# Finding an expert's rows in one-pass weights, the first expert's row numbers first, an early fetch that nothing uses, and the last statistics placed elsewhere in the queue

## The chip, the cores and the metric

One core of one Trainium2 chip. The metric is the device time of one launch in microseconds (us), median of the runs. TensorE multiplies, VectorE (DVE), ScalarE (ACT) and GpSimd (POOL) do the rest, SyncE (SP) issues most DMAs. Each engine runs its own list of instructions in order and waits on semaphores.

## What is computed

One step of a two-layer decoder trunk over 272 prompt positions (16 meta tokens and 256 new ones) and 32 sample tokens, all in float32, width 1024. Layer 0: pooling mixer and dense SwiGLU. Layer 1: conformer convolution and top-2-of-8 SwiGLU. Each sub-layer ends in a layer norm of 4**0.25 * x + f(x). The part that the change touches is the last sub-layer, for the 288 rows (256 prompt, 32 sample) that are handed out:

```
logits = xf @ router                       # (288, 8)
top_v, top_i = top_k(logits, 2); probs = softmax(top_v)
gate[t, e] = probability of expert e for row t, 0 if not chosen
y = sum over e of gate[:, e:e+1] * swiglu(xf, wg[e], wu[e], wd[e])
out = layer_norm(4**0.25 * xf + y)
```

## The kernel before

The work is laid out by hand: five engine programs, each a fixed order of instructions, tied by counting semaphores. Weights come in 1 MB tiles into a ring of eleven buffers (`raw`). ACT copies each tile into a rounded high part (`hi(t)`, L683) and DVE forms the low part (`lo(t)`, L1334), so that a product of float32 numbers is three matmuls on operands of type fp32r (L1075, L1106, L1243, L1267).

**Routing.** DVE takes the two largest of eight logits (`top_v`, `top_i`), makes masks `pick1`, `pick2`, `taken`, and TensorE counts with triangular matrices where each row stands in the list of its expert (L1196). `slot_of` holds this place. `select(e0, e1)` (L1648) compares it with 0 to 127 and writes for experts e0 to e1 a 0/1 matrix `sel` (rows by places). `find_rows` (L1211) multiplies `sel` with `gate`, which holds per row a one, the eight shares and the row's number, in float32: ten columns for each expert, three matmuls for each expert (rows in parts of 128, 128 and 32), in three groups `FINDS` (expert 0; 1 to 3; 4 to 7). `input_rows(k)` (L1658, L1660) copies row numbers into `row_in` and the rest into `found`; `output_rows` (L1678 to L1685) makes from it the shares and the rows to add to. Eight narrow-purpose matmuls in `mean_mat` follow (`keep_busy(8)`, L999, each two instructions in the trace).

**The first fetch.** POOL waits until the 288 rows are in DRAM (`rows_stored`, L507) and until `row_in` has expert 0's numbers, and fetches its rows by an indirect DMA (L616) into `xg_rows`. TensorE, once its own list has come to it, turns them (`gather_turn`, L1221), ACT and DVE split them (`xg_hi` L889, `xg_lo` L1715), and the first expert's matmuls start (L1243).

**An expert** has 33 tiles, in six blocks j = 0 to 5 (NB = 6). For each block TensorE multiplies by gate tiles, turns the hidden block j-1 (`turn_h`, L1252), multiplies by up tiles, and runs `down(j-1)` (L1267), which waits for DVE's `turn_low(j-1)` (`ht_lo`, L1739). Blocks 0 to 4 have two gate tiles, two up tiles and two down tiles; block 5 has one of each. `down(5)` stands behind all six blocks. DVE's order in block j is: two `lo` tiles, `turn_low(j-1)`, two `lo` tiles, `mult(j)` (`hn`, L1734), two `lo` tiles.

**The end.** All rows but those of expert 7 are finished while expert 7 runs. SP loads the sums of experts 0 to 6 into `acc` (L517, three DMAs, counted to 48 by `sums_loaded`), behind the last weight tiles and the rows of gains and biases. DVE, in expert 7, behind the last `lo` of block 4, waits for the 48 and does for the three parts of the rows `rows_stats` (L1692, L1695), then in block 5 `turn_low(4)`, `rows_center` (L1700) of two parts, `mult(5)`, the third centre, `rows_scale` (L1709) of two parts, `turn_low(5)` and the third scale. `last_rows` (L1789 to L1801) does the rows of expert 7, which POOL places in the outputs.

Of the kernel before, what the change touches and what calls it, by code (L numbers as in the profile page):

```python
# [24 lines left out]
F32 = mybir.dt.float32  # L25
# [15 lines left out]
def build_trunk(nc, x_prompt, x_sample, state_pool, state_conv, meta, pool_w, pool_scale, conv_w1,  # L41
# [57 lines left out]
    with ExitStack() as ctx:  # L99
# [40 lines left out]
        GC = E + 2  # L140
        gate = const("gate", [P, 3, GC])
        slot_of = const("slot_of", [P, 3, E + 1])
        trash = const("trash", [P, 2])
# [67 lines left out]
        sel = area("sel", [P, E, 3, P], F32, M0 + 12288)  # L211
# [9 lines left out]
        xg_lo = area("xg_lo", [P, KC, P], F32R, M1 + 4096)  # L221
        hn = area("hn", [P, BW], F32, M1 + 8192)
# [12 lines left out]
        found = area("found", [P, 1 + E * (GC + 1)], F32, 8576)  # L235
# [8 lines left out]
        def sem(name):  # L244
            return ctx.enter_context(nc.semaphore(name))
# [85 lines left out]
        rows_moved = sem("rows_moved")  # L331
        found_moved = sem("found_moved")
# [75 lines left out]
        FINDS = ((0, 1, 4), (1, 4, 5), (4, E, 6))  # L408
# [172 lines left out]
        def _(pool):  # L581
# [17 lines left out]
            pool.memset(gate[:], 0.0).then_inc(pool_step, 1)  # L599
# [5 lines left out]
            pool.memset(gate[:, :, 0:1], 1.0).then_inc(consts_ready, 1)  # L605
            pool.iota(gate[:, :, GC - 1:GC], pattern=[[P, 3], [1, 1]], base=0, channel_multiplier=1,
# [43 lines left out]
            with pool.If(largest > P):  # L650

                pool.indirect_dma_start(sums_dram, rows(row_out[:, E - 1:E], 0), yy[:], None).then_inc(added, 16)
                for r in (1, 2):
                    pool.wait_ge(in_ready, r * 3 + 3)
# [10 lines left out]
        N_CONSTS = 13  # L665
# [314 lines left out]
        def _(pe):  # L980
# [223 lines left out]
            def find_rows(r, k):  # L1204

                e0, e1, bank = FINDS[k]
                pe.wait_ge(sel_ready, r * len(FINDS) + (k + 1))
                for e in range(e0, e1):
                    for i in range(3):
                        n = OUT_ROWS[i]  # L1210
                        last = pe.matmul(ps[bank][:, GC * e:GC * (e + 1)], sel[0:n, e, i, :], gate[0:n, i, :],  # L1211
                                         start=(i == 0), stop=(i == 2))
                last.then_inc(rows_found, 1)
# [108 lines left out]
        def _(dve):  # L1322
# [28 lines left out]
            link(dve.tensor_scalar(recip[:], slot_no[:, 0:16], 1.0, None, ALU.add))  # L1351
            link(dve.reciprocal(recip[:], recip[:]))
# [277 lines left out]
            dve.wait_ge(placed, 1)  # L1630
            for i in range(3):
                last = dve.tensor_scalar(pick1[:, i, :], pick1[:, i, :], prob[:, i, 2:3], None, ALU.mult)
            link(last)
            for i in range(3):
                last = dve.scalar_tensor_tensor(out=slot_of[:, i, 0:E], in0=ps[1][:, i * E:(i + 1) * E], scalar=1.0,
                                                in1=taken[:, i, :], op0=ALU.add, op1=ALU.mult)
            for i in range(3):
                n = OUT_ROWS[i]
                last = dve.scalar_tensor_tensor(out=gate[0:n, i, 1:1 + E], in0=pick2[0:n, i, :],
                                                scalar=prob[0:n, i, 3:4], in1=pick1[0:n, i, :],  # L1640
                                                op0=ALU.mult, op1=ALU.add)
# [13 lines left out]
            def input_rows(k):  # L1655
                e0, e1, bank = FINDS[k]
                cols = slice(GC * e0, GC * e1)
                dve.tensor_copy(row_in[:, e0:e1], ps[bank][:, cols].rearrange("p (e c) -> p e c", c=GC)[:, :, GC - 1])\  # L1658
                    .then_inc(in_ready, 1)
                dve.tensor_copy(found[:, cols], ps[bank][:, cols]).then_inc(found_moved, 1)  # L1660
# [10 lines left out]
            for k in (1, 2):  # L1671
                dve.wait_ge(rows_found, k + 1)
                input_rows(k)

            def output_rows(r):

                dve.wait_ge(found_moved, r * len(FINDS) + len(FINDS))
                dve.tensor_scalar(row_f[:], found_at[:, :, 0], trash[:, 1:2], trash[:, 0:1], ALU.mult,  # L1678
                                  ALU.add).then_inc(rows_moved, 1)
                dve.tensor_copy(share[:], found[:, 1:].rearrange("p (e c) -> p e c", c=GC + 1)[:, :, 0])\  # L1680
                    .then_inc(rows_moved, 1)
# [37 lines left out]
            def one_expert(r, first, side, last):  # L1719
# [22 lines left out]
                for j in range(NB):  # L1742
                    a = FIRST[j] + AHEAD
                    ahead(a)
                    if halves(j) == 2:
                        ahead(a + 1)
                    if j:
                        turn_low(j - 1)
                    if halves(j) == 2:
                        ahead(a + 2)  # L1750
                        ahead(a + 3)
                    else:
                        ahead(a + 1)
# [9 lines left out]
                    if kept and j == NB - 2:  # L1763
                        dve.wait_ge(sums_loaded, 48)
                        for i in range(3):
# [59 lines left out]
            xg_low(0)  # L1825
            one_pass(0)
# [3 lines left out]
            with dve.If(largest > P):  # L1830
                dve.wait_ge(y_placed, 32)
                with dve.Fori(1, 3) as r:
# [7 lines left out]
                    for k in range(len(FINDS)):  # L1840
                        dve.wait_ge(rows_found, r * len(FINDS) + (k + 1))
                        input_rows(k)
# [41 lines left out]
```

## Time and profile before

| what | value |
|---|---|
| median of 3 runs | 1248.1 us (1248.07 to 1249.15) |
| the profiled execution's own time | 1249.45 us |
| its span, first to last instruction | 1247.7 us |
| TensorE busy / share of the span | 1206.4 us / 97% |
| VectorE, ScalarE, GpSimd busy | 975.4, 807.1, 31.9 us |
| mean granted TensorE clock | 0.989 |
| chain that ended last | PE 87%, DVE 9%, ACT 2%, DMA 1%, issue 1% |

The span is 1.75 us short of that execution's own time. TensorE is nearly always busy in the profile, but a busy TensorE may be one at a low clock or with very narrow operands, and the chain of what ended last leaves TensorE at places where another engine holds it up.

### The profile page before, as it was taken

The page shows a single profiled execution, that of the slowest core. Times are in us where ns is not written, and L with a number is a line of the kernel's source. Part 1 is how long each engine was busy: PE and PEld are TensorE (multiplying, and loading weights), DVE is VectorE, ACT ScalarE, POOL GpSimd, SP SyncE. Part 2 cuts the span into 40 slices and gives each one's busy share as a digit, 9 for nine tenths or more (in the row PEclk, how much of TensorE's full clock was granted, in tenths as well). Part 3 has the DMA queues.
Part 4 walks back from the last instruction along what each step waited for, and adds up shares of the span by engine and source line. Part 5 has one row for each costly group of instructions (what it writes and reads, how often), then busy time and mean ns, then how long its engine had stood idle before and what let it go on. Part 6 is the DMA issues. An engine that isn't in the chain of part 4 may idle for free.

```text
span 1247.7 us, 16144 instructions
## 1 busy us (share of the span) xinstructions
PE 1206.4 (97%) x6567; PEld 1045.6 (84%) x6567; DVE 975.4 (78%) x907; ACT 807.1 (65%) x875; POOL 31.9 (3%) x40
## 2 busy tenths in 40 slices
PE   6999999999998989999999999999999999999996
PEld 4899999999997878888888888888888888888885
DVE  6787444447898559889888888888888888888887
ACT  4545654436596448768767777777777777777771
POOL 0000000000000000001001001001001001001000
PEclk9999999999999979999999999999999999999998
DMA  9144544442193439999999999999999999999991
GB/s 257 41 151 153 169 145 160 141 156 90 53 318 107 135 110 327 366 366 359 385 371 359 388 368 356 393 374 358 391 367 348 394 376 342 394 380 344 395 345 50
DMA packets 171388, 345.74 MB, mean 277 GB/s; under 512 B 7042, under 2 KB 59618, under 8 KB 171274
## 3 DMA queue, kind: packets, MB, share of 16 engines
q1 hardware_dynamic: 168515, 335.34, 75.1%
q0 software_dynamic: 2592, 8.66, 2.8%
q8 instruction: 54, 0.88, 0.3%
q10 hardware_dynamic: 199, 0.62, 0.2%
q14 instruction: 28, 0.23, 0.1%
HBM read 336.34 MB, written 10.44 MB: 278 GB/s over the span
## 4 chain that ended last, share of the span: by engine, by line
PE 87%; DVE 9%; ACT 2%; DMA 1%; issue 1%; POOLq 0%; ACTq 0%; POOL 0%; DVEq 0%
PE bank L1243 39%; PE bank L1267 19%; PE bank L1075 18%; PE bank L1106 6%; DVE cacc L1517 3%; PE bank L1252 1%; PE bank L1014 1%; PE bank L1211 1%; DVE w_lo L1334 1%; DMA spool<-in_state_pool_dram 1%; PE bank L1060 1%; DVE sg L1414 1%; ACT w_hi L683 0%; ACT sq L727 0%; DVE cacc L1538 0%
## 5 line engine op out<-in xcount | busy, mean ns | idle before, releaser
L1334 DVE TENSOR_TENSOR w_lo<-raw,w_hi 128x2048 fp32r<-128x2048 f32 x309 | 704.5, 2290 | 164.8 <-ACT w_hi L683 163.8
L683 ACT CAST w_hi<-raw 128x2048 fp32r<-128x2048 f32 x309 | 589.5, 1916 | 243.2 <-PE bank L1243 81.3
L1243 PE MATMUL bank<-w_hi,xg_hi 128*128 128x512 f32 (+1 forms) x768 | 292.1, 380 | 1.1 <-DVE xg_lo L1715 1.1
L1243 PE MATMUL bank<-w_hi,xg_lo 128*128 128x512 f32 (+1 forms) x768 | 288.6, 376 | 0.0
L1243 PE MATMUL bank<-w_lo,xg_hi 128*128 128x512 f32 (+1 forms) x768 | 288.6, 376 | 0.0
L1075 PE MATMUL bank<-x_hi,w_hi 128*128 128x304 f32 (+1 forms) x544 | 166.8, 307 | 6.9 <-DVE x_lo L1421 3.7
L1243 PEld LDWEIGHTS bank<-w_hi,xg_hi 128*128 128x128 f32 x768 | 144.2, 188 | 29.2 <-issue 1.3
L1243 PEld LDWEIGHTS bank<-w_hi,xg_lo 128*128 128x128 f32 x768 | 144.2, 188 | 29.1
L1243 PEld LDWEIGHTS bank<-w_lo,xg_hi 128*128 128x128 f32 x768 | 144.4, 188 | 28.0
L1075 PE MATMUL bank<-x_lo,w_hi 128*128 128x304 f32 (+1 forms) x544 | 165.1, 304 | 0.0
L1075 PE MATMUL bank<-x_hi,w_lo 128*128 128x304 f32 (+1 forms) x544 | 164.5, 302 | 0.0
L1267 PE MATMUL bank<-w_hi,ht_hi 128*128 128x512 f32 x352 | 140.1, 398 | 1.7 <-DVE ht_lo L1739 1.4
L1267 PE MATMUL bank<-w_hi,ht_lo 128*128 128x512 f32 x352 | 139.2, 395 | 0.0
L1267 PE MATMUL bank<-w_lo,ht_hi 128*128 128x512 f32 x352 | 139.1, 395 | 0.0
L1075 PEld LDWEIGHTS bank<-x_hi,w_hi 128*128 128x128 f32 x544 | 103.2, 190 | 8.8 <-issue 6.3
L1075 PEld LDWEIGHTS bank<-x_hi,w_lo 128*128 128x128 f32 x544 | 103.2, 190 | 0.0
L1075 PEld LDWEIGHTS bank<-x_lo,w_hi 128*128 128x128 f32 x544 | 103.0, 189 | 0.1
L1267 PEld LDWEIGHTS bank<-w_hi,ht_hi 128*128 128x128 f32 x352 | 66.0, 188 | 19.1 <-DVE ht_lo L1739 3.8
L1267 PEld LDWEIGHTS bank<-w_hi,ht_lo 128*128 128x128 f32 x352 | 66.0, 188 | 16.1
L1267 PEld LDWEIGHTS bank<-w_lo,ht_hi 128*128 128x128 f32 x352 | 66.0, 188 | 15.3
L1106 PE MATMUL bank<-h_hi,w_hi 128*128 128x304 f32 x176 | 54.5, 310 | 1.9 <-DVE h_lo L1491 1.9
L1517 DVE SCALAR_TENSOR_TENSOR cacc<-uext,vec,cacc 128x256 f32<-128x256 f32 x134 | 53.9, 480 | 0.0
(206 smaller groups left out, 1097.0 us busy)
## 6 DMA issues: line engine op xcount, KB each, us to landing
raw<-in_moe_w_gate_dram SPq DMA_DIRECT2D x88, 1024.0 KB, 7.0
raw<-in_moe_w_up_dram SPq DMA_DIRECT2D x88, 1024.0 KB, 7.4
raw<-in_moe_w_down_dram SPq DMA_DIRECT2D x88, 1024.0 KB, 7.1
raw<-in_conv_w_dram SPq DMA_DIRECT2D x12, 1024.0 KB, 5.2
raw<-in_ffn_w_gate_dram SPq DMA_DIRECT2D x11, 1024.0 KB, 5.3
raw<-in_ffn_w_up_dram SPq DMA_DIRECT2D x11, 1024.0 KB, 5.3
raw<-in_ffn_w_down_dram SPq DMA_DIRECT2D x11, 1024.0 KB, 4.8
sums_dram<-acc SPq DMA_DIRECT2D x3, 512.0 KB, 3.0
```

Source lines behind the costliest of these rows:

```text
L683: act.copy(w_hi[t % HIGH][:], raw[raw_slot(t)][:]).then_inc(hi_ready, 1)
L1014: last = pe.matmul(ps[0][:, 0:n], mean_mat[:], z(c), start=(c == first), stop=(c == end))
L1060: last = pe.matmul(ps[1][:, 0:n], mean_mat[:], sq[:, c, 0:n], start=(c == 0), stop=(c == KC - 1))
L1075: last = pe.matmul(bank[:, 0:n], w[:, c, cols], x[:, c, 0:n], start=(c == 0 and k == 0), stop=(c == KC - 1 and k == 2))
L1106: last = pe.matmul(ps[c][:, 0:NT], w[:, s, cols], x[i % 2][:, s, :], start=(i == 0 and s == 0 and k == 0), stop=(i == NJ - 1 and s == TR - ...
L1211: last = pe.matmul(ps[bank][:, GC * e:GC * (e + 1)], sel[0:n, e, i, :], gate[0:n, i, :], start=(i == 0), stop=(i == 2))
L1243: done = pe.matmul(bank[:, 0:w], x[:, f, :], m[:, c, :], start=(f == 0 and k == 0), stop=(f == KC - 1 and k == 2))
L1252: done = pe.transpose(ps[4 + j % 2][:, s * P:(s + 1) * P], hn[:, s * P:(s + 1) * P], ident[:])
L1267: done = pe.matmul(ps[6 + half][:, :], x[:, i * TR + s, :], w[:, s, cols], start=(j == 0 and i == 0 and s == 0 and k == 0), stop=(j == NB ...
L1334: dve.tensor_tensor(w_lo[raw_slot(t)][:], raw[raw_slot(t)][:], w_hi[t % HIGH][:], ALU.subtract).then_inc(split_ready, 1)
L1414: link(dve.reciprocal(rs[:, 0:n], rs[:, 0:n]))
L1517: ins = dve.scalar_tensor_tensor(out=out, in0=src, scalar=v(V_DW + KC * k + q), in1=out, op0=ALU.mult, op1=ALU.add)
```

## The change

`gate` with its ten columns becomes `row_cols` with 18 columns of type fp32r: a one, the eight shares rounded, the eight remainders of the shares, and the row's number. `sel` is fp32r too, so `find_rows` multiplies fp32r by fp32r. `FINDS` has two groups of four experts. Ahead of them three matmuls of two columns (the row's number and its neighbour) find expert 0's row numbers alone. DVE no longer forms the shares before `slot_of`; it scales `pick1` before it waits for the places, forms `gate`, the rounded parts and the remainders between the first `select` and the others, and copies `row_in` for experts 1 to 7 in one go once both groups are found. `keep_busy(8)` becomes `keep_busy(4)`, behind a wait for `in_ready`. POOL fetches 128 rows of the prompt into an area that nothing reads (`hn_all`), once the statistics of the last norm ahead of the routing are done; DVE waits for its landing before the experts. At the start POOL writes one more constant and DVE copies the row numbers into `row_cols`. In expert 7 DVE waits for the sums, and does `rows_stats` of part 0, ahead of `turn_low(3)`; part 1 stands ahead of `mult(4)`; part 2 and the centres of parts 0 and 1 stand at the end of block 4; the centre of part 2 stands ahead of `mult(5)`, and all three scales ahead of `turn_low(5)`.

```diff
-        GC = E + 2
-        gate = const("gate", [P, 3, GC])
+        GC = 2 * E + 2
+        row_cols = const("row_cols", [P, 3, GC], F32R)
-        sel = area("sel", [P, E, 3, P], F32, M0 + 12288)
+        sel = area("sel", [P, E, 3, P], F32R, M0 + 12288)
-        FINDS = ((0, 1, 4), (1, 4, 5), (4, E, 6))
+        FINDS = ((0, E // 2, 5), (E // 2, E, 6))
...
+            pool.wait_ge(var_done, 4)
+            pool.indirect_dma_start(hn_all[:], None, x_prompt[0], rows(any_row[:], 0)).then_inc(warmed, 16)
             pool.wait_ge(rows_stored, 48)
             pool.wait_ge(in_ready, 1)
             fetch(0, 0)
-            pool.wait_ge(in_ready, 3)
+            pool.wait_ge(in_ready, 2)
...
-                pe.wait_ge(sel_ready, r * len(FINDS) + (k + 1))
+                pe.wait_ge(sel_ready, r * len(FINDS) + (k + 2))
...
+            pe.wait_ge(sel_ready, 1)
+            for i in range(3):
+                n = OUT_ROWS[i]
+                last = pe.matmul(ps[1][:, 0:2], sel[0:n, 0, i, :], row_cols[0:n, i, GC - 2:GC],
+                                 start=(i == 0), stop=(i == 2))
+            last.then_inc(first_found, 1)
             for k in range(len(FINDS)):
                 pe.wait_ge(acc_ready, FINDS[k][2] - 2)
                 find_rows(0, k)
-            keep_busy(8, bank=1)
+            pe.wait_ge(in_ready, 1)
+            keep_busy(4, bank=1)
...
-            dve.wait_ge(placed, 1)
             for i in range(3):
                 last = dve.tensor_scalar(pick1[:, i, :], pick1[:, i, :], prob[:, i, 2:3], None, ALU.mult)
             link(last)
+            dve.wait_ge(placed, 1)
...
             select(0, 1)
-            select(1, 4)
             dve.wait_ge(turned, T_XJ + len(X_JOBS))
-            dve.wait_ge(rows_found, 1)
-            input_rows(0)
-            select(4, E)
+            for i in range(3):
+                n = OUT_ROWS[i]
+                last = dve.scalar_tensor_tensor(out=gate[0:n, i, :], in0=pick2[0:n, i, :], scalar=prob[0:n, i, 3:4],
+                                                in1=pick1[0:n, i, :], op0=ALU.mult, op1=ALU.add)
+            last.then_inc(gate_step, 1)
+            dve.wait_ge(first_found, 1)
+            dve.tensor_copy(row_in[:, 0:1], ps[1][:, 1:2]).then_inc(in_ready, 1)
+            dve.wait_ge(gate_step, 1)
+            dve.tensor_copy(row_cols[:, 0:2, 1:1 + E], gate[:, 0:2, :])
+            dve.tensor_copy(row_cols[0:NS, 2, 1:1 + E], gate[0:NS, 2, :]).then_inc(gate_step, 1)
+            dve.wait_ge(gate_step, 2)
+            dve.tensor_tensor(row_cols[:, 0:2, 1 + E:1 + 2 * E], gate[:, 0:2, :], row_cols[:, 0:2, 1:1 + E], ALU.subtract)
+            dve.tensor_tensor(row_cols[0:NS, 2, 1 + E:1 + 2 * E], gate[0:NS, 2, :], row_cols[0:NS, 2, 1:1 + E],
+                              ALU.subtract).then_inc(gate_step, 1)
+            dve.wait_ge(gate_step, 3)
+            select(1, E // 2)
+            select(E // 2, E)
...
+                    if kept and j == NB - 2:
+                        dve.wait_ge(sums_loaded, 48)
+                        rows_stats(0, 0)
                     if j:
                         turn_low(j - 1)
...
+                    if kept and j == NB - 2:
+                        rows_stats(0, 1)
                     if kept and j == NB - 1:
-                        for i in range(2):
-                            rows_center(0, i)
+                        rows_center(0, 2)
                     mult(j)
...
                     if kept and j == NB - 2:
-                        dve.wait_ge(sums_loaded, 48)
-                        for i in range(3):
-                            rows_stats(0, i)
+                        rows_stats(0, 2)
                         dve.wait_ge(rows_landed, 32)
+                        for i in range(2):
+                            rows_center(0, i)
                 if kept:
-                    rows_center(0, 2)
-                    for i in range(2):
+                    for i in range(3):
                         rows_scale(0, i)
                 turn_low(NB - 1)
-                if kept:
-                    rows_scale(0, 2)
```

## Rows read from the trace of the kernel before

**Rows 1.** Chain of waits, 380 to 472 us: start us, us, engine, tile, line.
```profile
452.37 10.40 PE bank L1211 x42
462.78 3.42 PE bank L999 x16
...
468.12 3.97 PE bank L1243 x16
```

**Rows 2.** Timeline, 436 to 475 us: start us, us, engine, line, operation, tiles, [idle before].
```profile
447.91 0.17 DVE L1629 TENSOR_TENSOR prob<-prob 128x3 f32<-128x3 f32 x1
...
448.91 0.50 DVE L1632 TENSOR_SCALAR pick<-pick,prob 128x8 f32<-128x8 f32 x3 [0.83 <-PE bank L1196]
449.44 0.31 DVE L1635 SCALAR_TENSOR_TENSOR slot_of<-bank,taken 128x8 f32<-128x8 f32 x3
449.67 0.48 DVE L1639 SCALAR_TENSOR_TENSOR gate<-pick,prob,pick 128x8 f32<-128x8 f32 x3
...
450.40 1.83 DVE L1648 TENSOR_TENSOR sel<-slot_no,slot_of 128x384 f32<-128x384 f32 x2
...
451.10 0.90 PE L1211 MATMUL bank<-gate,sel 128*128 128x10 f32 x6 [1.45 <-DVE sel L1648]
452.14 0.15 DVE L1658 CAST row_in<-bank 128x1 uint32<-128x1 f32 x1
...
453.19 1.84 POOL L616 DMA_INDIRECT xg_rows<-rows_dram,row_in  x1 [169.06 <-DVE row_in L1658]
...
467.84 0.95 POOL L616 DMA_INDIRECT xg_rows<-rows_dram,row_in  x1 [12.80 <-PE bank L1221]
```

**Rows 3.** DMA issues, 452 to 462 us: queue, KB each, us from issue to landing.
```profile
xg_rows<-rows_dram,row_in POOLq DMA_INDIRECT x1, 5.3
```

**Rows 4.** Windows, routing: length, busy per engine, TensorE clock, DMA share, GB/s.
```profile
436.00:444.00 8.00, 6.61 (x39) 3.58 (x38) 7.84 (x11) 5.12 (x11) 0.00 (x0) 1.00 0.00 0
...
452.00:463.00 11.00, 10.63 (x44) 10.28 (x44) 2.71 (x10) 0.00 (x0) 1.84 (x1) 0.50 0.47 158
463.00:466.00 3.00, 3.00 (x16) 3.00 (x16) 0.79 (x5) 0.00 (x0) 0.00 (x0) 0.54 0.00 0
```

**Rows 5.** Windows, the convolution on TensorE: the same columns.
```profile
360.00:370.00 10.00, 10.00 (x87) 10.00 (x86) 10.00 (x32) 10.00 (x35) 0.00 (x0) 1.00 0.89 313
```

**Rows 6.** Windows, an idle stretch and the work behind it: the same columns.
```profile
46.70:48.50 1.80, 0.00 (x0) 0.02 (x1) 1.63 (x4) 0.99 (x2) 0.00 (x0) 1.00 0.01 5
49.40:52.60 3.20, 3.20 (x15) 3.20 (x14) 3.20 (x8) 1.83 (x4) 0.00 (x0) 0.50 0.00 0
```

**Rows 7.** Timeline of VectorE, last expert.
```profile
1207.74 2.29 DVE L1334 TENSOR_TENSOR w_lo<-raw,w_hi 128x2048 fp32r<-128x2048 f32 x1 [0.51 <-ACT w_hi L683]
1209.94 0.68 DVE L1739 TENSOR_TENSOR ht_lo<-bank,ht_hi 128x512 fp32r<-128x512 f32 x1
...
1215.97 0.68 DVE L1734 TENSOR_TENSOR hn<-sgn,bank 128x512 f32<-128x512 f32 x1
...
1221.56 1.28 DVE L1692 BATCH_NORM_STATS2 stats<-acc 128x6 f32<-128x512 f32 x2
...
1225.78 0.64 DVE L1739 TENSOR_TENSOR ht_lo<-bank,ht_hi 128x512 fp32r<-128x512 f32 x1
1226.34 2.47 DVE L1700 SCALAR_TENSOR_TENSOR acc<-acc,mv,g_row 128x1024 f32<-128x1024 f32 x2
```

**Rows 8.** Timeline of TensorE, last expert.
```profile
1214.36 0.40 PE L1267 MATMUL bank<-w_hi,ht_hi 128*128 128x512 f32 x1
...
1226.47 0.50 PE L1267 MATMUL bank<-w_hi,ht_hi 128*128 128x512 f32 x1 [0.31 <-DVE ht_lo L1739]
...
1233.64 0.50 PE L1267 MATMUL bank<-w_hi,ht_hi 128*128 128x512 f32 x1 [1.06 <-DVE ht_lo L1739]
```

**Rows 9.** Timeline of the SyncE queue, last expert.
```profile
1204.38 1.56 SPq L517 DMA_DIRECT2D acc<-sums_dram  x3
```

**Rows 10.** DMA issues, 1200 to 1210 us: queue, KB each, us from issue to landing.
```profile
acc<-sums_dram SPq DMA_DIRECT2D x1, 128.0 KB, 9.7
```

More of the change, by code:

```diff
@@ L234, in build_trunk @@
         stats = area("stats", [P, 4, 2, 6], F32, 8384)
-        found = area("found", [P, 1 + E * (GC + 1)], F32, 8576)
+        gate = area("gate", [P, 3, E], F32, 9280)
+        found = area("found", [P, 1 + E + E * (GC + 1)], F32, 8576)
+        assert 8576 + 4 * (1 + E + E * (GC + 1)) <= 9280
         rows_dram = nc.dram_tensor("rows_dram", (NM, D), F32, kind="Internal").ap()
@@ L331, in build_trunk @@
         rows_moved = sem("rows_moved")
+        warmed = sem("warmed")
+        first_found = sem("first_found")
+        gate_step = sem("gate_step")
         found_moved = sem("found_moved")
@@ L598, in _ @@
                 pool.memset(t[:], 0.0 if t is not slot_of else NEG).then_inc(consts_ready, 1)
-            pool.memset(gate[:], 0.0).then_inc(pool_step, 1)
+            pool.iota(any_row[:], pattern=[[1, 1]], base=0, channel_multiplier=1).then_inc(consts_ready, 1)
+            pool.memset(row_cols[:].bitcast(F32), 0.0).then_inc(pool_step, 1)
             pool.iota(trash[:, 0:1], pattern=[[1, 1]], base=NM, channel_multiplier=1,
@@ L604, in _ @@
             pool.wait_ge(pool_step, 3)
-            pool.memset(gate[:, :, 0:1], 1.0).then_inc(consts_ready, 1)
-            pool.iota(gate[:, :, GC - 1:GC], pattern=[[P, 3], [1, 1]], base=0, channel_multiplier=1,
+            pool.memset(row_cols[:, :, 0:1].bitcast(F32), 1.0).then_inc(consts_ready, 1)
+            pool.iota(trash[:, 2:5], pattern=[[P, 3]], base=0, channel_multiplier=1,
                       allow_small_or_imprecise_dtypes=True).then_inc(consts_ready, 1)
@@ L1210, in find_rows @@
                         n = OUT_ROWS[i]
-                        last = pe.matmul(ps[bank][:, GC * e:GC * (e + 1)], sel[0:n, e, i, :], gate[0:n, i, :],
+                        last = pe.matmul(ps[bank][:, GC * e:GC * (e + 1)], sel[0:n, e, i, :], row_cols[0:n, i, :],
                                          start=(i == 0), stop=(i == 2))
@@ L1636, in _ @@
                                                 in1=taken[:, i, :], op0=ALU.add, op1=ALU.mult)
-            for i in range(3):
[L1638 to L1641, printed above, removed]
             link(last)
@@ L1653, in _, with found_share @@
             found_row = found_at[:, :, GC - 1]
[L1655 to L1660, printed above, removed]
+            def found_share(c):
+                return found[:, c:c + E * (GC + 1)].rearrange("p (e c) -> p e c", c=GC + 1)[:, :, 0]
             select(0, 1)
-            select(1, 4)
             dve.wait_ge(turned, T_XJ + len(X_JOBS))
-            dve.wait_ge(rows_found, 1)
-            input_rows(0)
-            select(4, E)
+            for i in range(3):
[15 more added lines that the diff above has]
+            select(E // 2, E)
             dve.wait_ge(counted, 1)
@@ L1670, in _ @@
             dve.tensor_copy(most_i[:], most[:]).then_inc(flag_ready, 1)
-            for k in (1, 2):
-                dve.wait_ge(rows_found, k + 1)
-                input_rows(k)
+            dve.wait_ge(rows_found, 1)
+            dve.tensor_copy(found[:, 0:GC * (E // 2)], ps[5][:, 0:GC * (E // 2)]).then_inc(found_moved, 1)
+            dve.wait_ge(rows_found, 2)
+            dve.tensor_copy(found[:, GC * (E // 2):GC * E], ps[6][:, GC * (E // 2):GC * E]).then_inc(found_moved, 1)
+            dve.wait_ge(found_moved, 2)
+            dve.tensor_copy(row_in[:, 1:E], found_row[:, 1:E]).then_inc(in_ready, 1)
             def output_rows(r):
@@ L1679, in output_rows @@
                                   ALU.add).then_inc(rows_moved, 1)
-                dve.tensor_copy(share[:], found[:, 1:].rearrange("p (e c) -> p e c", c=GC + 1)[:, :, 0])\
-                    .then_inc(rows_moved, 1)
+                dve.tensor_tensor(share[:], found_share(1), found_share(1 + E), ALU.add).then_inc(rows_moved, 1)
                 dve.wait_ge(rows_moved, r * 3 + 2)
@@ L1839, in _ @@
                         select(e0, e1)
-                    for k in range(len(FINDS)):
+                    for k, (e0, e1, bank) in enumerate(FINDS):
                         dve.wait_ge(rows_found, r * len(FINDS) + (k + 1))
-                        input_rows(k)
+                        dve.tensor_copy(found[:, GC * e0:GC * e1], ps[bank][:, GC * e0:GC * e1]).then_inc(found_moved, 1)
+                    dve.wait_ge(found_moved, r * len(FINDS) + len(FINDS))
+                    dve.tensor_copy(row_in[:], found_row).then_inc(in_ready, 2)
                     output_rows(r)
```

11 lines of the change are left out of this document (7 added, 4 removed).

## The prediction, made before the changed kernel had run

> **What bounds the kernel now.** I read the page's busy shares first (TensorE 97%), then the chain of waits, to see at which places TensorE's time is not the matmuls of the weights. Two such places meet the change.
>
> The first is the routing. The chain there [rows 1] is all TensorE: 42 instructions of finding rows take 10.40 us, 16 of keep-busy 3.42, then the turn of the fetched rows, and the experts start at 468.12. The finds have ten columns, so they carry next to no work, yet they take 10.40 / 42 = 0.248 us each. The windows say why they are that slow: the granted clock is 0.50 from 452 to 463 us and 0.54 in the next three [rows 4], the lower level, 1.2 GHz, where the convolution ran at 1.00 [rows 5]. The first fetch is no bound: POOL starts it at 453.19 [rows 2] and it lands 5.3 us later [rows 3], at 458.5, while TensorE comes to the turn only at 462.78 + 3.42 = 466.2.
>
> The second is expert 7. TensorE waits for DVE's `turn_low` twice, 0.31 and 1.06 us [rows 8]. DVE's timeline [rows 7] is full: what DVE is given there, or made to wait for, goes on to TensorE. Between these two places lie seven experts bound by TensorE, which a shift passes through unchanged, so the two effects add.
>
> **The routing, step by step.** `pick1` is now scaled before the wait for `placed`. DVE's last step ahead of it ended at 447.91 + 0.17 = 448.08 and the scale takes 0.50, so it is done before 448.91, when the places came [rows 2]: 449.44 - 448.91 = 0.53 gone. `gate` leaves the stretch too, 0.4 of its 0.48. The first `select` starts 0.93 sooner, at 449.47. Finding started 0.70 behind it (451.10), so now at 450.17, and its three matmuls instead of six instructions end some 0.4 sooner than the 1.04 that passed until `row_in` (452.14). `row_in` is written at 450.8, POOL starts the fetch 1.05 later as before (453.19 - 452.14), at 451.85, and it lands by 457.2 even at the old 5.3.
>
> The warming fetch starts near 434, once the last norm's statistics are done. POOL has nothing to do then, and from 436 to 444 us the DMAs move nothing [rows 4]; that is its cover, and without it half a megabyte would cost about what the fetch costs, 5 us of a queue that nobody waits for. What it can give is the issue, 1.84 us for the first fetch and 0.95 for the second [rows 2]. That is 0.9 on a fetch that has 460.4 - 457.2 = 3 us of slack behind TensorE. I cost it at nothing; below nothing is excluded by the same slack.
>
> DVE then has two casts and two subtractions of 8 or 16 columns, like its small steps of 0.15 to 0.18: 0.5 us with the links, so `select` of experts 1 to 3 starts at 451.4. A pair of selects for four experts took 1.83, 0.46 each, so they are ready at 452.8 and those of 4 to 7 at 454.6. TensorE now starts the main finds at 452.9.
>
> How long they take the trace doesn't show: no fp32r matmul of few columns is in it. The number of instructions falls from 48 to 24 (plus three), since fp32r goes in one where float32 takes two, as [rows 2] has six for three calls. Each is bounded by 0.115 us from below (the convolution, 87 in 10 us at the full clock [rows 5]) and 0.248 from above. At the low clock, which I expect to last (TensorE has even less to do here), twice 0.115 is 0.23, and both rows meet: I take 0.24. So 24 x 0.24 = 5.8, finds end at 458.7; eight instructions of keep-busy at 3.42 / 16 = 0.214 are 1.7, 460.4. From there to the first expert matmul it took 468.12 - 466.2 = 1.9, with the clock just risen; at the low clock four of the transposes in that path take 0.4 more. The experts start at 462.7, **5.4 us sooner**. `output_rows` is done by 460, earlier than needed. At 0.115 each, DVE's selects and the fetch bind instead: turn at 457.1, experts at 459.0, 9.1 sooner. At 0.248 it is 5.2.
>
> The clock then: keep-busy ran from 462.8, and a clock of 0.54 over 463 to 466 [rows 4] means that it rose 0.24 us before the end, at 465.76: 3 us. Now it runs 1.7 and the transposes 1.7, so the clock may not have risen when the experts start. A wait behind a norm shows the price: TensorE idle at 46.7 to 48.5, the clock at 0.50 from 49.4 to 52.6 [rows 6], during which 3.2 us of matmuls do 1.6 us of work. Ends: 0, and 1.6; I take half, **+0.8**.
>
> The start: one more constant on POOL and one small copy on DVE stand in front of inputs that are still being loaded; nothing, and at most the copy's 0.15.
>
> **Expert 7, step by step.** DVE now waits for all three loads of `acc` ahead of `turn_low(3)`. When have they landed? SP issues them from 1204.38 on for 1.56 us [rows 9], behind the last weight tiles and the two rows of gains, and the last one lands 9.7 us after its issue [rows 10] at 1205.5: 1215.2. That order is unchanged. DVE comes to the wait at 1209.94 [rows 7], so it stands still for 5.3 us. Queued behind are `turn_low(3)`, for which TensorE's `down(3)` waits, due at 1214.36 [rows 8], four `lo` tiles and `mult(4)`. Counting from 1215.2: one `rows_stats` (1225.78 - 1221.56 = 4.22 for three, 1.41 each), `turn_low(3)` 0.56 to the next instruction, four `lo` at 1209.94 - 1207.74 = 2.2 each, two more `rows_stats` 2.8, `mult(4)` 0.6, two centres 2.4, and from the start of `turn_low(4)` to TensorE 1226.47 - 1225.78 = 0.7. That sums to 1.4 + 0.6 + 8.8 + 2.8 + 0.6 + 2.4 + 0.7 = 17.3: `down(4)` starts at 1232.5, where it started at 1226.47. **+6.0 us.** `down(3)` slips to 1217.3, but TensorE has slack behind it: the work up to `down(4)` took 1226.47 - 0.31 - 1214.36 = 11.8, so it is through at 1229.1. From `down(4)` to `down(5)` 1233.64 - 1226.47 = 7.2 passed, so `down(5)` is due at 1239.7. DVE meanwhile has the third centre, `mult(5)` and three scales, each of the size of a centre with a reciprocal (1.2 + 0.4 + 3 x 1.45): through at 1238.5, so `turn_low(5)` is late by nothing; it may save up to 0.2 of the old 1.06, or cost 0.3 if a scale runs over. The third scale, gone from behind `turn_low(5)`, saves nothing, since `last_rows` waits for TensorE. The step's bounds are 5.7 and 6.5, by these and by the links between pieces.
>
> TensorE idles 3 us before `down(3)` and over 3 before `down(4)`. After 1.8 us of idling the clock fell [rows 6]. If it falls here, `down(4)` and what follows run slow for up to 3.2 us, at 1.6; part of a low stretch falls into the idling. Ends 0 and 1.6, I take **+1.2**.
>
> **Sum.** -5.4 + 0.8 + 6.0 + 1.2 = +2.6. Against the profiled execution's span that is 1250.3, its own time 1252.05; the median lies 1.35 below that execution, so 1248.1 + 2.6 = **1250.7**.
>
> **The rivals.** Beside the forecast (A, chance 0.50, own range 1248.8 to 1252.8):
>
> B, quick finds (0.15): the clock is at 1.00 in them, or one costs nearer 0.115. Front -9.1, tail +6.6: 1245.6. For it: fewer instructions. Against it: the clock fell and stayed low with more of them [rows 4].
>
> C, no stall in expert 7 (0.12), the one on the other side: the three sums are there when DVE asks. Then the stats and centres move into DVE's small idle places, `down(4)` starts within 0.5 of its time, and -4.6 + 0 gives 1243.5. It decides if the last landing comes before 1209.94, 5.3 us sooner than now; at 2.6 us sooner the whole is even with before. Against it: nothing issues them sooner.
>
> D, the clock stays low on into expert 0 (0.13): the transposes of the gather don't bring it up, and keep-busy is too short, so it rises only on expert matmuls, another 3.2 us at half speed, +1.6: 1252.3. For it: in 10.40 us of finds it never rose, though TensorE was busy 0.97 of the time [rows 4], so being busy is not enough. The Trainium skill, "TensorE: Matmul & The Clock Gate", Part 4: PE-mode transpose, says that transposes don't count as TensorE being busy in the way matmuls do; by it only the 1.7 us of keep-busy would help. The trace has no clock that rises on transposes alone, nor one that fails to.
>
> E, two passes in fp32r too (0.05): 48 x 0.248 = 11.9, experts start 0.6 later than before, +7.8: 1255.9. The weights' matmuls, once in the records for each call, speak against it.
>
> The rest, 0.05, is anything else, both ways.
>
> **Range and chances.** Under 0.2% (2.5 us) nothing can be told from no change. Leaving out C and E and a little more: 1245.6 to 1253.2. Slower: 0.30 of A, all of D and E, 0.02 of the rest, 0.50. Faster: C, 0.05 of B and 0.01, 0.18. Within: 0.32.
>
> **What would show it.** Right: 27 finds in one instruction each near 0.24 us at clock 0.50; POOL's fetch about 1.3 us sooner and 0.95 long; the first L1243 near 462.7; DVE idle some 5 us in expert 7 until the sums land; `down(4)` idle by over 3 us. Wrong: finds at 0.12 us, sums that land before DVE asks, or a first expert at half clock for many matmuls.

## The result and the profile after

The changed kernel took 1254.88 us, the median of four runs (1253.32 to 1257.67), against 1248.09 of before (1247.98 to 1249.15, four runs). The ratio is 1.0051, 95% interval 1.0038 to 1.0063: slower by half a percent. The profiled execution was the quickest of the four, 1253.32 us with a span of 1251.6; that of before had 1249.45 and 1247.7. The forecast was 1250.7, slower, and the time lies 1.7 us above its range. The two places that it named are there: expert 7 with the size that it gave, the routing 1.2 us short of it. What it left out lies between them.

The routing comes first. The chain of waits in the trace of the changed kernel, 440 to 475 us (start, us, what), answers to [rows 1]:

```profile
451.53 6.71 PE bank L1222 x24
458.24 2.00 PE bank L1010 x8
460.24 0.87 PE bank L1232 x4
...
462.59 12.64 PE bank L1254 x53
```

The timeline of the same stretch answers to [rows 2], and the DMA issues to [rows 3]:

```profile
444.19 2.23 SPq L514 DMA_DIRECT2D rows_dram<-xn  x3
...
448.18 0.56 DVE L1662 TENSOR_TENSOR sel<-slot_no,slot_of 128x384 fp32r<-128x384 f32 x1
...
449.41 0.16 DVE L1681 CAST row_in<-bank 128x1 uint32<-128x1 f32 x1 [0.27 <-PE bank L1320]
...
450.35 1.85 POOL L624 DMA_INDIRECT xg_rows<-rows_dram,row_in  x1 [14.97 <-DVE row_in L1681]
...
451.53 6.71 PE L1222 MATMUL bank<-row_cols,sel 128*128 128x18 f32 x24 [2.16 <-DVE sel L1662]
```

```profile
xg_rows<-rows_dram,row_in POOLq DMA_INDIRECT x1, 6.9
```

The first expert matmul is at 462.59, 5.53 us ahead of [rows 1]. Some of that is older than the routing. The rows' store, which stands ahead of it, is issued at 444.19; in the profile of before it was at 445.48, 1.29 later:

```profile
445.48 2.23 SPq L507 DMA_DIRECT2D rows_dram<-xn  x3
```

In the profile of before the clock was low for 3.4 us near 50 us [rows 6]; in this one it was 1.00 from 49.4 to 52.6, and the product that was running there, 1056 matmuls, took 148.32 us for 149.63. So this 1.3 us is a difference of the two executions, not of the kernels. The routing itself gave 5.53 - 1.29 = 4.2 us.

The windows (length, busy time of each engine, granted clock, DMA share, GB/s) show the clock in the finds, in expert 0 and in `down(3)` of expert 7:

```profile
450.90:461.10 10.20, 9.57 (x37) 9.20 (x38) 3.63 (x11) 0.00 (x0) 1.30 (x1) 0.50 0.48 163
461.20:470.00 8.80, 7.85 (x36) 6.23 (x35) 7.12 (x5) 8.80 (x8) 0.94 (x1) 1.00 0.54 177
1215.50:1218.90 3.40, 3.40 (x9) 2.67 (x9) 3.40 (x2) 0.00 (x0) 0.00 (x0) 0.51 0.00 0
```

Then expert 7. First DVE, then TensorE, the timelines that answer to [rows 7, 8]:

```profile
1205.60 2.29 DVE L1352 TENSOR_TENSOR w_lo<-raw,w_hi 128x2048 fp32r<-128x2048 f32 x1 [0.52 <-ACT w_hi L694]
1213.09 1.28 DVE L1718 BATCH_NORM_STATS2 stats<-acc 128x6 f32<-128x512 f32 x2 [5.20 <-DMA acc<-sums_dram]
...
1214.53 0.64 DVE L1765 TENSOR_TENSOR ht_lo<-bank,ht_hi 128x512 fp32r<-128x512 f32 x1
...
1227.32 2.43 DVE L1726 SCALAR_TENSOR_TENSOR acc<-acc,mv,g_row 128x1024 f32<-128x1024 f32 x2
1229.67 0.68 DVE L1765 TENSOR_TENSOR ht_lo<-bank,ht_hi 128x512 fp32r<-128x512 f32 x1
```

```profile
1215.22 0.54 PE L1278 MATMUL bank<-w_hi,ht_hi 128*128 128x512 f32 x1 [2.81 <-DVE ht_lo L1765]
...
1230.41 0.51 PE L1278 MATMUL bank<-w_hi,ht_hi 128*128 128x512 f32 x1 [1.67 <-DVE ht_lo L1765]
...
1237.45 0.50 PE L1278 MATMUL bank<-w_hi,ht_hi 128*128 128x512 f32 x1 [0.92 <-DVE ht_lo L1765]
```

DVE stands still for 5.20 us behind the last load of the sums. `down(3)` was due at 1215.22 - 2.81 = 1212.41; `down(4)` starts 18.0 us later, where in [rows 8] it was 1226.47 - 1214.36 = 12.1: 5.9 us lost. The last wait, 0.92 for 1.06, gives 0.1 back. The clock was low in `down(3)` (0.51 in the third window), where it cost nothing: TensorE would only have waited longer for `turn_low(4)`.

The difference of the spans is 1251.6 - 1247.7 = 3.9 us. Routing and the start give -5.5, expert 7 costs +5.8. That leaves +3.6 us between them, from the first expert matmul to `down(3)` of expert 7 (1212.41 - 462.59 = 749.8 against 1214.36 - 468.12 = 746.2), which the forecast took to pass a shift through unchanged. POOL's fetches in the middle of the run, one for each expert, show it. Before:

```profile
657.44 0.99 POOL L616 DMA_INDIRECT xg_rows<-rows_dram,row_in  x1 [87.73 <-PE bank L1221]
...
753.39 0.98 POOL L616 DMA_INDIRECT xg_rows<-rows_dram,row_in  x1 [87.77 <-PE bank L1221]
```

After:

```profile
652.81 0.98 POOL L624 DMA_INDIRECT xg_rows<-rows_dram,row_in  x1 [88.19 <-PE bank L1232]
...
749.18 0.98 POOL L624 DMA_INDIRECT xg_rows<-rows_dram,row_in  x1 [88.17 <-PE bank L1232]
```

An expert takes 96.37 us where it took 95.95 (96.36 to 96.43 over the run), at a granted clock of 1.00 in both. It isn't waiting either: from 556 to 1200 us TensorE is busy for 643.66 of the 644 us, and for 643.67 in before. The matmuls themselves are slower, as the chains of waits show for a pair of gate or up tiles (L1243, now L1254) and a pair of down tiles (L1267, now L1278), 24 matmuls in a row. Before, then after:

```profile
581.55 5.59 PE bank L1243 x24
587.15 5.60 PE bank L1267 x24
```

```profile
576.55 5.62 PE bank L1254 x24
582.17 5.62 PE bank L1278 x24
```

In layer 0, and in the convolution's first product, the pace is that of before: 513 matmuls of the down product took 72.07 us for 72.06, and 384 took 54.26 for 54.28. A chip that is slower throughout doesn't explain it. In these two products the weights are the stationary operand (the one that TensorE loads ahead of a matmul); they lie ahead of the constants and did not move. The activations that stream past them did move, and cost nothing by it. In the expert matmuls it is the other way round: the activations are stationary and the weights stream.

The medians differ by 6.8 us, the two profiled executions by 3.9. Of the 2.9 between, 1.3 is the low clock near 50 us. No profile of the change shows the rest; the profiled execution is its quickest, and the experiments show two places where others of its kind lose time to the clock.

### The profile page after: what moved, and what is told of

Same layout as the page of the kernel before. It is cut to its first block, busy times and chain, and to the rows that moved or that the text cites. A ratio compares the mean times of both kernels' runs of the same rounds, so it can differ in the third digit from the quotient of the medians.

```text
span 1251.6 us, 16090 instructions
## 1 busy us (share of the span) xinstructions
PE 1205.2 (96%) x6538; PEld 1043.3 (83%) x6538; DVE 976.2 (78%) x910; ACT 807.2 (64%) x875; POOL 31.8 (3%) x42
## 4 chain that ended last, share of the span: by engine, by line
PE 86%; DVE 9%; ACT 2%; DMA 1%; issue 1%; SPq 0%; POOLq 0%; POOL 0%; DVEq 0%; ACTq 0%
PE bank L1254 38%; PE bank L1278 19%; PE bank L1086 18%; PE bank L1117 6%; DVE cacc L1536 3%; PE bank L1263 1%; DVE w_lo L1352 1%; PE bank L1025 1%; DMA acc<-sums_dram 1%; PE bank L1071 1%; DVE sg L1433 1%; PE bank L1222 1%; DMA xin<-in_x_prompt_dram 0%; ACT sq L738 0%; DVE cacc L1557 0%
## 5 line engine op out<-in xcount | busy, mean ns | idle before, releaser
L1254 PE MATMUL bank<-w_hi,xg_hi 128*128 128x512 f32 (+1 forms) x768 | 293.0, 381 | 0.9 <-DVE xg_lo L1741 0.9
L1254 PE MATMUL bank<-w_hi,xg_lo 128*128 128x512 f32 (+1 forms) x768 | 289.6, 377 | 0.0
L1254 PE MATMUL bank<-w_lo,xg_hi 128*128 128x512 f32 (+1 forms) x768 | 289.5, 377 | 0.0
L1254 PEld LDWEIGHTS bank<-w_hi,xg_hi 128*128 128x128 f32 x768 | 144.7, 188 | 29.4 <-issue 1.2
L1254 PEld LDWEIGHTS bank<-w_hi,xg_lo 128*128 128x128 f32 x768 | 144.5, 188 | 29.4
L1254 PEld LDWEIGHTS bank<-w_lo,xg_hi 128*128 128x128 f32 x768 | 144.7, 188 | 28.2
L1278 PE MATMUL bank<-w_hi,ht_hi 128*128 128x512 f32 x352 | 141.1, 401 | 5.7 <-DVE ht_lo L1765 5.4
L1278 PE MATMUL bank<-w_hi,ht_lo 128*128 128x512 f32 x352 | 140.2, 398 | 0.0
L1278 PE MATMUL bank<-w_lo,ht_hi 128*128 128x512 f32 x352 | 140.1, 398 | 0.0
L1278 PEld LDWEIGHTS bank<-w_hi,ht_hi 128*128 128x128 f32 x352 | 66.7, 189 | 23.8 <-DVE ht_lo L1765 8.3
L1278 PEld LDWEIGHTS bank<-w_hi,ht_lo 128*128 128x128 f32 x352 | 66.8, 190 | 16.2
L1278 PEld LDWEIGHTS bank<-w_lo,ht_hi 128*128 128x128 f32 x352 | 66.7, 189 | 15.6
```

Source lines behind the costliest of these rows:

```text
L1254: done = pe.matmul(bank[:, 0:w], x[:, f, :], m[:, c, :], start=(f == 0 and k == 0), stop=(f == KC - 1 and k == 2))
L1278: done = pe.matmul(ps[6 + half][:, :], x[:, i * TR + s, :], w[:, s, cols], start=(j == 0 and i == 0 and s == 0 and k == 0), stop=(j == NB ...
```

## The experiments

Two theories stood at the outset. **Place in SBUF:** the change makes the constants larger (18 columns for ten and one more constant; the three more columns of `trash` fit into its padding), in all 128 bytes for each partition, and every tile laid out behind them moves up by that, the gathered rows and the turned hidden blocks among them, which the expert matmuls have as stationary operands. **Chip or run:** the longer period belongs to the chip that ran it. Beside these, the forecast's two places had to be shown apart. Each line of the table is a kernel against the runs of before in the same job.

| kernel | median us | ratio to before, 95% interval | expert period us |
|---|---|---|---|
| the change | 1254.88 | 1.0051 (1.0038 to 1.0063) | 96.37 |
| e1_front_only | 1249.23 | 1.0001 (0.9992 to 1.0010) | 96.37 |
| e2_tail_only | 1256.23 | 1.0048 (1.0034 to 1.0062) | 96.00 |
| e3_pad128 | 1252.21 | 1.0024 (1.0014 to 1.0035) | 96.37 |
| e4_after_packed | 1252.21 | 1.0025 (1.0015 to 1.0034) | 95.97 |
| e5_front_packed | 1244.98 | 0.9964 (0.9950 to 0.9977) | 95.95 |
| e6_xg_up128 | 1250.04 | 1.0006 (0.9997 to 1.0016) | 96.16 |
| e7_front_aligned | 1245.13 | 0.9965 (0.9951 to 0.9978) | 95.76 to 95.99 |
| e8_sums_later | 1249.07 | 0.9994 (0.9985 to 1.0003) | 96.00 |
| e9_no_warming | 1245.63 | 0.9971 (0.9962 to 0.9980) | 95.95 |
| e10_keep8 | 1246.20 | 0.9980 (0.9971 to 0.9989) | 95.95 |
| e11_finds_fp32 | 1250.15 | 1.0007 (0.9998 to 1.0016) | 95.97 |

Before was 1248.09 us beside the change, 1249.2 (24 runs) beside e1 to e4, 1249.5 (21 runs) beside e5 to e8 and 1248.59 (27 runs) beside e9 to e11. So kernels of different jobs are compared by their ratios. Periods are differences of fetch starts in each kernel's profile.

**e1_front_only: the change with expert 7's old order.**

```diff
-                    if kept and j == NB - 2:
-                        dve.wait_ge(sums_loaded, 48)
-                        rows_stats(0, 0)
                     if j:
                         turn_low(j - 1)
```
(and the other statistics, the centres and the scales back where they were)

> The changed kernel with expert 7's order of before put back; the routing part alone. Theory 'two places': the changed kernel's trace has the first expert matmul 5.5 us sooner, of which 1.3 are a low clock near 50 us that its run did not have, so the routing gives about 4.3, and expert 7's wait for the sums costs it back. By that theory this kernel loses no time in expert 7 (down(4) idles 0.3, down(5) about 1 us) and is 4 us faster than before, 1244, if the experts take 95.94 us each. Rival 'slower experts': the changed kernel's experts take 96.41 each where they took 95.94; if that comes with the routing part (its larger constants move every tile behind them by 128 bytes), it takes 8 x 0.46 = 3.7 back and this kernel is at 1247.5 to 1248.

Measured 1.0001, period 96.37: the rival. In its profile the first expert matmul is at 462.91, so the gain of the routing is there, and the slower experts eat it.

**e2_tail_only: before with expert 7's new order**, the same lines the other way round.

> The kernel before with the new order of statistics, centres and scales in expert 7 alone. Theory 'two places': DVE idles 5 us for the sums, down(3) starts some 3 us late, down(4) up to 6 us late: +4 (as in the changed kernel's trace: 15.0 us from down(3)'s due time 1212.4 to down(4) plus the rest, against 12.1) to +7.2 with a low clock: 1252 to 1255, experts at 95.94. Rival 'the wait is hidden': within 1 us of before.

Measured 1.0048, 6.0 us by the ratio and 7.0 by the medians, period 96.00: within the forecast's +4 to +7.2, though 1256.23 lies above its 1255. The wait is not hidden. TensorE's timeline and windows of its profile say how it gets there:

```profile
1218.28 0.50 PE L1267 MATMUL bank<-w_hi,ht_hi 128*128 128x512 f32 x1 [3.30 <-DVE ht_lo L1739]
...
1233.46 0.56 PE L1267 MATMUL bank<-w_hi,ht_hi 128*128 128x512 f32 x1 [3.27 <-DVE ht_lo L1739]
...
1242.01 0.50 PE L1267 MATMUL bank<-w_hi,ht_hi 128*128 128x512 f32 x1 [0.92 <-DVE ht_lo L1739]
```

```profile
1233.60:1237.00 3.40, 3.40 (x9) 2.66 (x10) 3.19 (x6) 0.00 (x0) 0.00 (x0) 0.52 0.00 0
```

Two idle stretches of 3.3 us, and `down(4)` starts at the lower level of the clock and takes 8.55 us to `down(5)` where [rows 8] have 7.17. Its five runs lie at 1254.6 twice, 1256.2 and 1257.9 twice; the profiled one is among the slowest.

**e3_pad128: 128 unused bytes behind the constants of before.**

```diff
+        place[0] += 128
         work = place[0]
```

> The kernel before with 128 unused bytes behind its constants, so that every tile behind them lies 128 bytes higher, as in the changed kernel; nothing else. Theory 'place in SBUF': the expert period (fetch to fetch) goes from 95.94 to 96.4 and the kernel is 3.3 to 3.7 us slower, 1251.6. Rival 'another chip or run': the period stays what the kernel before has on the same chip, and the time too.

Measured 1.0024, 3 us where 3.3 to 3.7 were expected; period 96.37, where e2 has 96.00 on the same chip, and a pair of tiles as in the changed kernel:

```profile
581.24 5.62 PE bank L1244 x24
586.85 5.62 PE bank L1268 x24
```

Only addresses differ from before. The place in SBUF is the cause, and 'chip or run' is out.

**e4_after_packed: the change with its small constants in one tile.**

```diff
-        eps = const("eps", [P, 1])
+        scal = const("scal", [P, 16])
+        eps = scal[:, 0:1]
+        most = scal[:, 1:2]
+        most_i = scal[:, 2:3].bitcast(I32)
+        any_row = scal[:, 3:4].bitcast(U32)
+        trash = scal[:, 4:9]
+        std3 = scal[:, 9:14]
```
(and their own tiles gone, so that all behind the constants lies where it lay in before)

> The changed kernel with its small constants packed into one tile of 64 bytes, so that everything behind the constants lies where it lay before. Theory 'place in SBUF': expert period 95.94, 3.3 to 3.7 us less than the changed kernel, about 1250 to 1251. Rival 'another chip or run', or a cause in the routing part itself: no less than the changed kernel on this chip.

Measured 1.0025 for the change's 1.0051, period 95.97: the same 3 us from the other side (2.7 by the medians). The time itself, 1252.21, lies 1.2 above the expected 1250 to 1251.

**e5_front_packed: e4 with expert 7's old order.**

> The changed kernel with expert 7's order of before and with its small constants packed, so that all behind them lies where it lay before: the routing part with neither of the two costs found. If the parts add as measured (the front alone 1.0001 of before with its expert period at 96.37; the packing 2.7 us less at an equal kernel, period 95.96), it is 1249.2 - 2.7 to 3.3 = 1246 to 1246.5, 0.998 of before, the first version that beats both. Rival 'the parts don't add': 1249 again.

Measured 0.9964: both costs out, the gain of the routing is left, 4.5 us, 1 to 1.5 more than expected. This kernel beats both. It also showed a term of the forecast that the change's own profile had not: in its profile the clock is still low when expert 0 begins.

```profile
464.65:468.50 3.85, 3.85 (x9) 3.11 (x10) 2.66 (x2) 3.85 (x3) 0.94 (x1) 0.50 0.46 136
```

Nine matmuls in 3.85 us, 0.43 each for 0.23; the clock rises near 469.2. From the first expert matmul (464.65) to expert 1's fetch it is 95.42 us, for 93.37 in before: 2.0 us. (From fetch to fetch it is 95.31 for 93.65, 1.7, but expert 0's fetch had itself slipped behind the slow transposes.) Of the seven profiles with four keep-busy matmuls and fp32r finds (the change, e1, e4, e5, e7, e8, e9) four have this: e5, e7, e8 and e9. The kernels of e4 and e5 are the same up to expert 7, and one has it and the other not, so it comes and goes between executions.

**e6_xg_up128: in before, the gathered rows' parts alone 128 bytes off.**

```diff
-        xg_hi = area("xg_hi", [P, KC, P], F32R, M1)
-        xg_lo = area("xg_lo", [P, KC, P], F32R, M1 + 4096)
+        xg_hi = area("xg_hi", [P, KC, P], F32R, M1 + 128)
+        xg_lo = area("xg_lo", [P, KC, P], F32R, M1 + 16384 + 128)
```

> The kernel before with only the gathered rows' high and low parts, the stationary operands of the gate and up matmuls, 128 bytes off their place modulo 256; the turned hidden blocks and all else stay. Theory 'the stationary operand's place': a gate or up tile of 24 matmuls takes 5.62 or more a pair-tile where 5.59 was, 288 of an expert's 420 matmuls are of this kind, so the period grows by 0.29 of the 0.42, to 96.2, and the time by 2 us. Rival 'another tile's place (the turned hidden blocks, or what DVE and ACT write)': period 95.95, no change.

(`xg_lo` goes to free space 12288 bytes further on, so that it overlaps nothing; modulo 512 it too lies 128 bytes higher.) The period is 96.16, half of the way and a little less than the 96.2 expected, and the chain tells which half:

```profile
580.22 5.62 PE bank L1243 x24
585.84 5.59 PE bank L1267 x24
```

The matmuls with the moved tile as stationary operand (L1243) have the slow pace, those with the turned hidden blocks (L1267), which stayed, the quick one. The time, 1.0006 with an interval down to 0.9997, is too close to 1 to bear this alone; the periods agree to 0.01 us from one expert to the next, and they do.

**e7_front_aligned: e5 with this group 160 bytes up, at a multiple of 512.**

```diff
-        M1 = M0 + 36864
+        M1 = M0 + 36864 + 160
```

> The same kernel as the front part with packed constants, but with the gathered rows, the hidden blocks and their turned parts moved up by 160 bytes, so that they begin at a multiple of 512 bytes. Theory 'the stationary operand's place', if it is about rows that start off a boundary: the period falls below 95.95, perhaps by another 0.4 an expert, 3 us in all. Rival 'only two levels': 95.96 or 96.37.

No further gain in time, 0.9965 for 0.9964. The periods are 95.98 early in the run and 95.76 from 750 us on, where 24 matmuls take 5.57 or 5.58 us, quicker than in any other run shown here. Four experts at 0.2 less would be 0.8 us, which the interval of the ratio doesn't resolve. No run has a reason for the step, so 'a boundary' is neither shown nor ruled out; 95.76 is neither of the rival's two levels.

**e8_sums_later: e4 with the wait for the sums, and the first statistics, where the sums have landed.**

```diff
-                    if kept and j == NB - 2:
-                        dve.wait_ge(sums_loaded, 48)
-                        rows_stats(0, 0)
                     if j:
                         turn_low(j - 1)
...
                     if kept and j == NB - 2:
+                        dve.wait_ge(sums_loaded, 48)
+                        rows_stats(0, 0)
                         rows_stats(0, 1)
```

> The changed kernel with packed constants and in expert 7 only the wait for the sums and the first part's statistics put behind turn_low(3) and the two tiles that follow it, where the sums have landed (they land 5 us behind DVE's arrival in the changed kernel); centres and scales stay as changed. Theory 'the wait costs': DVE doesn't idle, down(3) starts on time, and of the 6 us only what the two centres ahead of turn_low(4) cost is left: down(4) starts 1.8 to 2.4 us late, so the kernel is 3.7 to 4 us faster than the changed one with packed constants (1252.2), 1248.3. Rival 'it is the order of statistics and centres, not the wait': less than 1.5 us faster.

Measured 0.9994 for 1.0025: 3.9 us back by the ratios, 3.1 by the medians, for 3.7 to 4 expected. Its timeline has the statistics without a wait, and `turn_low(4)` only behind the centres:

```profile
1214.47 1.28 DVE L1719 BATCH_NORM_STATS2 stats<-acc 128x6 f32<-128x512 f32 x2
...
1223.70 2.43 DVE L1727 SCALAR_TENSOR_TENSOR acc<-acc,mv,g_row 128x1024 f32<-128x1024 f32 x2
1226.05 0.68 DVE L1766 TENSOR_TENSOR ht_lo<-bank,ht_hi 128x512 fp32r<-128x512 f32 x1
```

`down(4)` then idles 2.12 us and starts at the low clock (TensorE's timeline, and windows with a granted clock of 0.52):

```profile
1226.79 0.80 PE L1279 MATMUL bank<-w_hi,ht_hi 128*128 128x512 f32 x1 [2.12 <-DVE ht_lo L1766]
```

```profile
1226.70:1230.20 3.50, 3.41 (x8) 2.75 (x9) 3.29 (x7) 0.00 (x0) 0.00 (x0) 0.52 0.00 0
```

So the stall is some half of expert 7's loss. The rest is 0.9994 against e5's 0.9964, 3.7 us. This profile accounts for 3.1 of it: `down(4)` starts 13.9 us behind `down(3)` for 12.1 in [rows 8], with the centres ahead of `turn_low(4)`, and `down(5)` 8.49 behind `down(4)` for 7.17, at the low clock. No run moves the centres alone.

**e9_no_warming: e5 without the warming fetch.**

```diff
-            pool.wait_ge(var_done, 4)
-            pool.indirect_dma_start(hn_all[:], None, x_prompt[0], rows(any_row[:], 0)).then_inc(warmed, 16)
```
(and DVE's wait for it)

> The routing part with packed constants and expert 7's order of before (0.9964 of before), without the warming fetch and DVE's wait for it; nothing else. In the changed kernel's trace the first fetch that counts took 1.85 us to issue, as in before, so the warming fetch gave nothing; TensorE has slack over its landing anyway. Theory 'no effect': issue still 1.85 us, time within 1 us of the version with it, 1245 to 1246. Rival 'it warms something': issue longer than 1.85 us, later landing, a slower kernel.

No effect: 0.9971 for 0.9964, with intervals that overlap. The first fetch takes 1.93 us to issue without it and 1.85 with it, the next one 0.94 in both:

```profile
451.36 1.93 POOL L625 DMA_INDIRECT xg_rows<-rows_dram,row_in  x1 [167.61 <-DVE row_in L1680]
...
463.60 0.94 POOL L625 DMA_INDIRECT xg_rows<-rows_dram,row_in  x1 [10.31 <-PE bank L1231]
```

**e10_keep8: e5 with `keep_busy(8)`.**

> The same routing part with eight keep-busy matmuls instead of four. They cost eight more instructions at 0.22 to 0.26 us, 1.9 us, ahead of the turn of the fetched rows, if the clock is at its lower level throughout. Against it, they can bring the clock up before expert 0: in two of the seven profiles with four of them the first expert matmuls were still at the lower level for up to 3.4 us, 1.7 us of loss. Theory 'keep-busy is only cost': 1 to 1.9 us slower, 0.9975. Rival 'the clock pays it back': within 0.7 us.

(The count in that text is wrong: at the time it was three of six.) Measured 0.9980. Against e5's 0.9964, from another job, that is 2 us slower; against e9's 0.9971, in the same job, 1.1 by the ratios and 0.6 by the medians (1246.20 and 1245.63), with intervals that overlap. So the runs don't decide between the two theories. The profile shows both sides: expert 0 runs at the full clock and its fetch distance is 93.28 us, but keep-busy takes 3.78 us where four take 2.08. Those 1.7 are paid in each execution, the 2.0 of the clock only in some.

**e11_finds_fp32: e5 with `row_cols` and `sel` in float32.**

```diff
-        row_cols = const("row_cols", [P, 3, GC], F32R)
+        row_cols = const("row_cols", [P, 3, GC], F32)
-        sel = area("sel", [P, E, 3, P], F32R, M0 + 12288)
+        sel = area("sel", [P, E, 3, P], F32, M0 + 12288)
```

> The same routing part with the 0/1 matrices and the columns in float32, so that each find is two instructions again, of 18 columns (the remainders are then zero). Finds at 0.28 us each in one instruction took 6.71 us; at two of 0.25 each they take 12, so the turn comes 5.2 us later and the gain of the routing part (4.5 us) is gone: 1250, 1.000 to 1.001. This tells how much of the gain is the one pass. Rival 'the order of the steps gives it': 1 us or less lost.

Measured 1.0007: all of the gain gone, 4.5 us against e9 in the same job. The timeline has the finds in 48 instructions:

```profile
453.04 12.10 PE L1223 MATMUL bank<-row_cols,sel 128*128 128x18 f32 x48 [2.16 <-DVE sel L1663]
```

12.10 us for 6.71. The one pass carries the gain; with the order of the steps kept and two passes put back, nothing is left. That the early row numbers give nothing fits the fetch's slack ahead of TensorE, 3 us in the change, but no run has them alone.

## Why the prediction was wrong

The sign and the two named places were right. **The step that failed** is the sentence "Between these two places lie seven experts bound by TensorE, which a shift passes through unchanged, so the two effects add." A shift in time does pass; a shift in place doesn't. The change's first lines enlarge two constants, the layout puts everything behind them 128 bytes higher, and each expert takes 0.42 us longer: 3.6 us of the profile, 3.0 in e3, 2.7 to 3.3 between the change and e4. With 3.0 to 3.6 the sum would have been 1253.7 to 1254.3, and with the 1.2 that the finds and keep-busy took beyond their terms, 1254.9 to 1255.5; measured were 1254.88. Without the 3.0 to 3.6 the measured time would have been 1251.3 to 1251.9, inside the range. It was not among the rivals either, since the list of what the change does had no line for where tiles come to lie.

Point by point:

- **First select 0.93 sooner:** 0.93 (448.18 against 450.40 - 1.29). Right. `row_in` came at 449.41, 1.44 sooner than 452.14 - 1.29; forecast 1.3.
- **Finds 24 x 0.24 = 5.8:** mis-sized. They took 6.71, 0.28 each, above the upper end of 0.248. That bound was taken from float32 passes of ten columns; one fp32r instruction of 18 columns at the low clock cost more than one of them, though less than two (0.25 each with 18 columns in e11). Keep-busy took 2.0 for 1.7.
- **Routing -5.4:** -4.2, the 1.2 by these two.
- **Clock into expert 0, +0.8:** nothing in the profile of the change, 2.0 us in four of seven profiles, a little above the upper end of 1.6. The mean of the seven, 1.2, is not far from the half that was taken. Rival D has the mechanism of those four, but counts another 1.6 on top of the 0.8, 2.4 in all, and gave it a chance of 0.13: the case came more often and cost less. Whether the transposes brought the clock up is open: in the change it rose near 461.2, while they ran, and in e5 near 469.2, long after them. The Trainium skill, "TensorE: Matmul & The Clock Gate", Part 4: PE-mode transpose, says that a transpose doesn't count as TensorE being busy in the way a matmul does; e5 fits that, and no run here shows it.
- **Rival B's 1245.6:** its tail of +6.6 has no working; with the forecast's own 6.0 + 1.2 it would be 1246.2. The finds show no quick case, so nothing hangs on it.
- **Warming fetch at nothing:** right (e9). The reason was half wrong: it named a possible 0.9 us of issue that the slack would hide, and the issue stays at 1.85 us.
- **Fetch lands by 457.2:** mis-sized. 450.35 + 6.9 = 457.25 is 458.5 on the time scale of before (1.29 later), no sooner than in before: it started sooner but took 6.9 us for 5.3. It was not the bound: TensorE came at 460.2, which is 461.5 there.
- **Expert 7, +6.0:** +5.9 for `down(4)`, -0.1 at `down(5)`. DVE idled 5.20 us for a forecast of 5.3. Right, and shown by e2 and e8.
- **Clock in expert 7, +1.2:** in the profile it fell in `down(3)` (the third window above), where the slack hid it: `down(4)` idled 1.67 and not over 3. In e2 it fell in `down(4)` and cost 1.4. That may be part of the spread of the change, 1253.3 to 1257.7, but it was only seen in the profiles of other kernels.

## What to carry over

A diff that changes the size of one tile changes the place of all that are laid out behind it: list where the operands of the dominant matmuls come to lie before calling them unchanged, and test it with a padding of the old kernel, which costs one line. A wait put ahead in an engine's order is priced at the landing of what it waits for, and that could be read from the trace of before to a tenth (5.3 us forecast, 5.20 measured). A change of several parts can hide a good one: here the new routing gives 0.36% (e5), and two other parts take it away and more. A part that shows in some executions only, like the low clock in expert 0, needs more than one profile to be priced.

## What was not expected of the hardware

- An fp32r matmul of 128x512 went every 5.59 / 24 = 0.233 us or every 5.62 / 24 = 0.234, by the place of its stationary operand in SBUF. Moving it by 128 bytes does it (e3, e6), and only for the matmuls that read it (e6). Moving the streamed operand by as much did nothing in layer 0 (72.07 us for 72.06). Why is open. With a start at a multiple of 512 bytes (e7) the pace was 5.60 in the first experts and 5.57 to 5.58 in the last.
- With 18 columns, at the low clock, one fp32r instruction took 0.28 us (6.71 / 24) and one float32 instruction 0.25 (12.10 / 48).
- The first indirect fetch took 1.85 us to issue, whether another had run 16 us earlier or not (e9), and the later ones 0.94. At 1.85 the DMAs are storing `sums_dram`; that the two are linked is a guess, and wasn't tried.
